# The X form of a blockwise triangular inverse kept in PSUM by an identity product, the other form added by VectorE

## What is computed

```
def step(S, inp):
    r_t, w_t, k_t, v_t, kk_t, a_t = inp
    sa = jnp.einsum('bhvk,bhk->bhv', S, -kk_t)
    S = S * w_t[:, :, None, :] + sa[..., None] * (kk_t * a_t)[:, :, None, :] + v_t[..., None] * k_t[:, :, None, :]
    return S, jnp.einsum('bhvk,bhk->bhv', S, r_t)
```

## Time and profile before

| | us |
|---|---|
| median of 3 runs (870.77 to 873.72) | 873.22 |
| the profiled execution itself | 872.92 |
| its span, first to last instruction | 871.1 |
| PE busy | 815.2 |
| DVE busy | 494.8 |
| ACT busy | 330.9 |
| RWKV stage, 222.9 to 357 us of the span | 134.1 |

### The profile page before, as it was taken

One profiled execution on the slowest core, in us unless ns is written; L12 is line 12 of the kernel. 1 busy time (PEld: TensorE's weight loads), 2 busy tenths in 40 slices (PEclk: granted clock), 3 DMA queues, 4 the chain that ended last, 5 costly groups with the idle time before them and its releaser, 6 DMA issues.

```text
span 871.1 us, 23141 instructions
## 1 busy us (share of the span) xinstructions
PE 815.2 (94%) x10012; PEld 763.6 (88%) x10012; DVE 494.8 (57%) x764; ACT 330.9 (38%) x569; POOL 274.0 (31%) x121
## 2 busy tenths in 40 slices
PE   6999999999887777899998999999999999999994
PEld 6899889898677676688888999999999999999994
DVE  5588766786577666265354777766667661000037
ACT  5644565454313122433265434333333331111124
POOL 0000000000297670325252444444344434344300
PEclk9999999999999999999998999999999999999997
DMA  7232133152243343703111333223322332333202
GB/s 267 84 97 74 49 98 98 49 198 61 88 116 107 107 126 118 237 15 104 58 54 44 98 113 106 80 91 98 97 86 85 98 88 89 92 88 89 85 2 99
DMA packets 32470, 83.47 MB, mean 96 GB/s; under 512 B 5144, under 2 KB 10456, under 8 KB 31728
## 3 DMA queue, kind: packets, MB, share of 16 engines
q1 hardware_dynamic: 32368, 81.98, 30.7%
HBM read 75.87 MB, written 5.91 MB: 94 GB/s over the span
## 4 chain that ended last, share of the span: by engine, by line
PE 86%; DVE 7%; ACT 3%; issue 2%; POOL 1%; DMA 0%; DVEq 0%; ACTq 0%; POOLq 0%
PE banks L1850 83%; PE banks L1904 1%; DVE z L1241 1%; DVE xx L1241 1%; PE banks L2253 1%; DVE ms L1241 1%; DVE rw L1241 1%; DVE z L1244 1%; POOL wr_lo L697 1%; DVE ssa L1505 1%; ACT x_hi L1149 0%; ACT z L1152 0%; ACT z L1212 0%; DMA w_raw<-in_w 0%; ACT nv L982 0%
## 5 line engine op out<-in xcount | busy, mean ns | idle before, releaser
L1850 PE MATMUL banks<-x_hi,w_hi 128*128 128x264 f32 (+1 forms) x784 | 207.7, 298 | 11.4 <-DVE x_lo L1241 8.9
L1850 PE MATMUL banks<-x_hi,w_lo 128*128 128x264 f32 (+1 forms) x784 | 198.3, 286 | 0.0
L1850 PE MATMUL banks<-x_lo,w_hi 128*128 128x264 f32 (+1 forms) x784 | 198.3, 286 | 0.0
L1850 PEld LDWEIGHTS banks<-x_hi,w_hi 128*128 128x128 f32 x784 | 138.9, 191 | 24.5 <-issue 11.3
L1850 PEld LDWEIGHTS banks<-x_lo,w_hi 128*128 128x128 f32 x784 | 139.1, 192 | 0.1
L1850 PEld LDWEIGHTS banks<-x_hi,w_lo 128*128 128x128 f32 x784 | 138.9, 191 | 0.0
L697 POOL TENSOR_TENSOR w_lo<-w_raw,w_hi 128x1024 fp32r<-128x1024 f32 (+1 forms) x38 | 90.6, 2385 | 152.2 <-ACT w_hi L825 152.0
L697 POOL TENSOR_TENSOR wx_lo<-w_raw,wx_hi 128x1024 fp32r<-128x1024 f32 (+1 forms) x34 | 81.8, 2406 | 100.5 <-ACT wx_hi L825 100.1
L1244 DVE SCALAR_TENSOR_TENSOR z<-z,banks 128x260 f32<-128x260 f32 (+1 forms) x24 | 12.4, 515 | 122.1 <-PE banks L1850 121.9
L1850 PE MATMUL banks<-x_hi,wx_lo 128*128 128x260 f32 x352 | 73.5, 283 | 0.0
L1850 PE MATMUL banks<-x_hi,wx_hi 128*128 128x260 f32 x352 | 73.5, 282 | 0.0
(11 more groups left out here) (254 smaller groups left out, 1713.0 us busy)
## 6 DMA issues: line engine op xcount, KB each, us to landing
w_raw<-in_w SPq DMA_DIRECT2D x87, 512.0 KB, 3.6
w_raw<-in_w SPq DMA_DIRECT2D x16, 448.0 KB, 3.3
kv<-in_ck SPq DMA_DIRECT2D x16, 192.0 KB, 4.1
kv<-in_cv SPq DMA_DIRECT2D x16, 192.0 KB, 3.4
att<-in_x SPq DMA_DIRECT2D x8, 264.0 KB, 6.0
att_out<-att SPq DMA_DIRECT2D x1, 2112.0 KB, 8.9
z<-in_xc SPq DMA_DIRECT2D x2, 1040.0 KB, 6.7
y_out<-z SPq DMA_DIRECT2D x8, 260.0 KB, 2.2
```

Of the source, the lines that this page charges most:

```text
L1850: return pe.matmul(out, l, r, start=start, stop=stop)
```

## The change

The masks of levels 1 to 5 change sign, so that the update adds where it subtracted. On PE a new `keep(n, l, g)` stands right after both groups of `half_products`, for l = 1..4: for each partition half j one matmul of the identity with form 1 of four heads (256 columns) starts an accumulation in bank 4g+1; the level's form-1 products are then added to it there. DVE's `update` treats only form 0 (128x256). ACT's new `x_copy(n, l)` copies form 1 back, 128x256 per group. At l = 5 nothing of this kind is kept, and DVE's `xf` waits for the copy. The copies are put into ACT's list; the `vb` activations (L1032), `ssoft`, `sprob` and `wu_copy` keep their order, with copies between. Four semaphores are merged into others: `zeroed` for two zeroing flags, `bsel_landed` counts `own_head` too, and `sel_landed` counts `gate_up`, so that `gate(0)` waits for three transfers and not one.

```
+    lev[:, 1:NLEV] *= -1
...
+        def x_copy(n, l):
+            for g in range(2):
+                ac.wait_ge(d_ps, (NLEV - 1) * 2 * n + 2 * (l - 1) + g + 1)
+                ac.activation(xx[:, 4 * g:4 * g + 4, 1, :], banks[:, 4 * g + 1, 256:512].rearrange("p (h s) -> p h s", h=4),
+                              ACT.Copy).then_inc(xg_done, 1)
+                own(xg_done)
...
-        for tb in range(1, TB):
-            vt_copy(tb)
+        vt_copy(1)
+        x_copy(0, 1)
+        vt_copy(2)
+        vt_copy(3)
+        for l in range(2, NLEV - 1):
+            x_copy(0, l)
...
                 b1_copy(n - 1)
+                x_copy(n, 1)
...
                 wu_copy(n - 1)
+                x_copy(n, 2)
+                if n == TB - 1:
+                    ac.wait_ge(s_pback, 1)
...
+                x_copy(n, 3)
                 if n == 1:
                     for c in range(CC):
...
                     token_copy(n, 0)
+                x_copy(n, 4)
                 ny_copy(n - 1)
...
-                x = xx[:, hs, :, :].rearrange("p h a s -> p a h s")
-                tt(x, x, banks[:, 4 * g:4 * g + 2, 256:512].rearrange("p a (h s) -> p a h s", h=4), ALU.subtract)\
+                tt(xx[:, hs, 0, :], xx[:, hs, 0, :], banks[:, 4 * g, 256:512].rearrange("p (h s) -> p h s", h=4), ALU.add)\
                     .then_inc(d_done, 1)
             else:
+                ve.wait_ge(xg_done, 2 * (NLEV - 2) * (n + 1))
...
-                   ALU.subtract).then_inc(d_done, 1)
+                   ALU.add).then_inc(d_done, 1)
...
+        def keep(n, l, g):
+
+            if l > 1:
+                pe.wait_ge(xg_done, 2 * ((NLEV - 2) * n + l - 2) + g + 1)
+            for j in range(2):
+                mm(banks[rows(j), 4 * g + 1, 256:512], level[rows(j), NLEV, :], xx[rows(j), 4 * g:4 * g + 4, 1, :], True, False)
...
-                    ins = mm(banks[rows(j), 4 * g + 1, o], lower[rows(j), h, 1, :], xx[rows(j), h, 1, :])
-                    if l < NLEV - 1:
+                    ins = mm(banks[rows(j), 4 * g + 1, o], lower[rows(j), h, 1, :], xx[rows(j), h, 1, :], last, last or i == 3)
+                    if not last:
...
                     half_products(n, l)
+                if l < NLEV - 1:
+                    keep(n, l, 0)
+                    keep(n, l, 1)
...
-                pe.wait_ge(gate_landed, 16)
+                pe.wait_ge(sel_landed, 48)
```

More of the change, by code:

```diff
@@ L127, in shape_constants @@
     lev[:, NLEV] = k[:, None] == t[None, :]
+    before, upto = k[:, None] < t[None, :], k[:, None] <= t[None, :]
+    lev[:, 1:NLEV] *= -1
     c["level"] = lev
-    before, upto = k[:, None] < t[None, :], k[:, None] <= t[None, :]
     c["causal"] = np.concatenate([before, upto, before, -lev[:, 0]], 1).astype(np.float32)
@@ L333, in layer @@
     late_landed = sem("late_landed")
-    gate_landed = sem("gate_landed")
     bsel_landed = sem("bsel_landed")
-    own_landed = sem("own_landed")
     x_hi_ready = sem("x_hi_ready")
@@ L340, in layer @@
     rw_ready = sem("rw_ready")
-    pre_zero = sem("pre_zero")
+    zeroed = sem("zeroed")
     v_tok_ps = sem("v_tok_ps")
@@ L354, in layer @@
     att_left = sem("att_left")
-    kv_zero = sem("kv_zero")
     s_rows_ps = sem("s_rows_ps")
@@ L413, in layer @@
     d_done = sem("d_done")
+    xg_done = sem("xg_done")
     b1_ps = sem("b1_ps")
@@ L542, in keys_of @@
             r = b % NKV
-            sp.wait_ge(kv_zero, min(b, NKV - 1) + 1)
+            sp.wait_ge(zeroed, min(b, NKV - 1) + 2)
             if b >= NKV:
@@ L608, in _ @@
         sp.wait_ge(n_spread, CC)
-        sp.dma_start(low_up[:], a["own_head"]).then_inc(own_landed, 16)
+        sp.dma_start(low_up[:], a["own_head"]).then_inc(bsel_landed, 16)
         sp.wait_ge(w_hi_ready, N_IN)
@@ L647, in _ @@
         sp.wait_ge(att_left, 16)
-        sp.dma_start(gate_up[:], a["gate_up"]).then_inc(gate_landed, 16)
+        sp.dma_start(gate_up[:], a["gate_up"]).then_inc(sel_landed, 16)
         sp.dma_start(gsel[:], a["gsel"]).then_inc(sel_landed, 16)
@@ L699, in w_low @@
             own(w_late_ready)
-        pool.memset(pre[:, :, 0:1], 0.0).then_inc(pre_zero, 1)
-        own(pre_zero)
+        pool.memset(pre[:, :, 0:1], 0.0).then_inc(zeroed, 1)
+        own(zeroed)
         pool.wait_ge(slot_used, N_IN)
         for r in range(NKV):
-            pool.memset(kv[96:P, r * NSB * AW:(r + 1) * NSB * AW], 0.0).then_inc(kv_zero, 1)
-            own(kv_zero)
+            pool.memset(kv[96:P, r * NSB * AW:(r + 1) * NSB * AW], 0.0).then_inc(zeroed, 1)
+            own(zeroed)
         def products(b):
@@ L826, in late_high @@
             own(w_hi_ready)
-        ac.wait_ge(pre_zero, 1)
+        ac.wait_ge(zeroed, 1)
         ac.activation(pre[:, 1, 0:1], pre[:, 1, 0:1], ACT.Copy)
@@ L1028, in _ @@
                 wu_copy(n - 1)
+                x_copy(n, 2)
+                if n == TB - 1:
+                    ac.wait_ge(s_pback, 1)
+                    ac.activation(sprob[:, :, :], banks[:, 7, 0:NSB * B * H].rearrange("p (t n) -> p t n", t=NSB),
+                                  ACT.Copy).then_inc(s_prob, 1)
+                    own(s_prob)
+                x_copy(n, 3)
                 if n == 1:
@@ L1493, in own_heads @@
         def own_heads(g):
-            ve.wait_ge(own_landed, 16)
+            ve.wait_ge(bsel_landed, 32)
             ve.wait_ge(s_pv, NSB * (g + 1))
@@ L2061, in inverse_scores @@
                 pe.wait_ge(p_done, 2 * (NLEV - 1) * n - 1 + g)
+                pe.wait_ge(xg_done, 2 * (NLEV - 2) * n - 1 + g)
             for i in range(2):
@@ L2137, in full_products @@
             pe.wait_ge(p_done, k + 1)
-            if l == NLEV - 1 and n + 1 < TB:
+            last = l == NLEV - 1
+            if last:
+                pe.wait_ge(xg_done, 2 * (NLEV - 2) * n + 2 * (NLEV - 2) - 1 + g)
+            if last and n + 1 < TB:
                 pe.wait_ge(sc_ps, 2 * n + g + 3)
@@ L2411, in gn_spread @@
             if u == 0:
-                pe.wait_ge(sel_landed, 32)
+                pe.wait_ge(sel_landed, 48)
             pe.wait_ge(n_inv, RT_G + u + 1)
```

## The result

The median after is 876.43 us (874.61 to 879.25, 17 runs) against 871.47 (867.81 to 874.91, 17 runs) for the kernel before: ratio 1.0057, 95% interval [1.0043, 1.0071], slower by 5.0 us. The forecast was 879.2, slower by 6.0 than the 873.2 of the runs shown then. The profiled execution took 878.41, 5.5 more than that of before (872.92); both are slower than their kernel's median, by 2.0 and 1.5 us.

A forecast was written before the change was run, and what follows sets the result against it. It took a dependency chain hopping between PE and DVE as the stage's bound. Added 11.4 us minus 5.1 gained gave +6.3, less 0.2 for a stall: 873.2 + 6.1, say 879.2 us; range 870.0 to 882.5.

The forecast's parts named there:

- What bounds the stage: A dependency chain hopping between PE and DVE; the end of PE's inserted key_scores and value_scores releases DVE's masks.
- Price of `keep`: Identity products on PE behind the half products, ahead of the inserted work: 0.85 us per level, 11.4 us in all.
- The gain: Shorter DVE updates after levels 1, 2, 3: 0.27 + 0.54 + 0.54 per step n = 1 to 3; 5.1 us in all.
- n = 0: First step: keep adds 2.43 us over levels 1 to 4; levels 1 and 2 gain 0.54 each.
- Level 4 of n = 1: PE restarts at a low clock after 2.71 us idle and is itself the bound; keep costs 1.3 us there.
- The stall: A 0.43 us issue stall between level 2's two groups; added pauses may shrink it, so 0.2 us taken off.
- Rival 1: Levels 1 to 3: keep is covered on free array quarters and only the gain remains, 868 us; chance 0.15.
- the forecast's second rule: PSUM evacuation: using both ScalarE and VectorE is advised; by it the sum would be the 5.1 us gain alone.
- Rival 2: Low-clock stretches: added PE work keeps the clock up, saving 4.7 us at most, no change at 873.8; chance 0.12.
- Rival 3: keep costs double, from quarters in turn or a new low-clock stretch per step: about 21 us, 889; chance 0.06.
- ACT's copies and the merged waits: 32 ACT copies, 12.3 us of ACT work, and gate(0) waiting for three transfers: cost 0 on the path.

The follow-up runs named there:

- The late version: The changed kernel with keep moved from behind the half products to just ahead of the full products; 0.9997 of the kernel before, 872.32 us.
- `keep` alone: The kernel before with keep's identity products added behind the half products, their result overwritten, DVE and ACT unchanged; ratio 1.0098, 881.40 us.
- the gain alone: The changed kernel without keep, so the inverse is not computed; ratio 0.9975 to the kernel before, 870.43 us.
- the shifted runs: Tiny products at kernel start: kernel before with 32, 876.11 us, with 64, 873.35; changed kernel with 32, 879.37; with keep also ahead of full products, 879.52.

## Why the prediction was right, and which terms were off

- **What bounds the stage.** Right: the release of the masks by PE's inserted work, ahead of the updates. The late version shows it by taking 0.83 us back at the mask with the same work on PE. (The 0.022 us a record that the forecast worked out from the earlier trace rows counts only the 95 records on the chain; the stretch holds 113, so 0.018. It supports the same conclusion, that the quarters run side by side.)
- **Price of `keep`.** 0.85 us a level was taken from the identity products of the start; measured 0.83 at level 1. Exposed at level 1 and 2, as forecast. From level 2 to 3 the sum of price and gain should have been 0.85 - 0.54 = +0.31 and was +0.16, so 0.7 of the 0.85 was exposed there, as the 0.68 of `keep` alone says too. Alone, the price was 8.5 us and not 11.4.
- **The gain.** 0.27 + 0.54 + 0.54 a step: shown at level 4 (-0.52, the forecast's -0.54) and in the gain alone (0.26, 0.52 and 0.52). So a step of n >= 1 should come to +1.20 by the forecast (1.35 gained, 2.55 added) and came to +1.07.
- **n = 0.** +1.35 forecast (2.43 less 1.08), +0.88 measured.
- **Level 4 of n = 1.** 1.3 us for work at half clock. This term failed as put: the low stretch it rests on was not there. The same view of after at 272.2 us, and at two other stretches:

```profile
272.20:279.00 6.80, 5.49 (x255) 4.91 (x256) 5.34 (x11) 4.48 (x8) 6.52 (x3) 1.00 0.14 44
...
284.00:287.00 3.00, 3.00 (x62) 2.67 (x62) 1.02 (x2) 0.64 (x2) 0.00 (x0) 0.50 0.69 217
...
356.00:360.00 4.00, 4.00 (x61) 3.55 (x59) 2.13 (x7) 1.92 (x3) 3.49 (x2) 0.50 1.08 316
```

  The granted clock at 272.2 is 1.00 (2.4 GHz) and is 0.50 (1.2 GHz) later, at 284, after a stretch in which PE stood still for issue and for DVE, and again at 356, behind the 3.95 us stall. In the stage as a whole it is 0.95, where the earlier trace rows have 0.96. What level 4 of n = 1 cost can't be read, since a stall (0.49) lies in it.
- **The stall.** The forecast knew of one, of 0.43 us, and took 0.2 off for "added pauses before it". This step failed: the chain of before had 5.8 us of such pieces in the stage, and the profiled execution of after 9.95. They are no pause that shrinks but late instruction blocks, and adding 128 PE and 128 PEld records to the stage moved their boundaries. Moved boundaries alone do not explain the rise: the last stall lies at nearly the same place in both (318 records before the output projection in before, 324 in after) and took 3.95 us instead of 2.71. That the time came out so near the forecast (+5.0 for +6.0) is in part luck: the measured levels gave +4.1 where the forecast had +5.0 for them (its +6.3 less the 1.3 of level 4 of n = 1), and stalls and clock, for which it had nothing like their size, can move a version by 3 us and more, as the shifted runs show.
- **Rivals.** Rival 1 (`keep` covered, 868) falls by the row of 2.88 against 2.05; the gain alone, which this rival and the forecast's second rule would leave, is not what came. The Trainium skill ("TensorEngine Tiling (Array Packing)", section PSUM Bottleneck) advises to use both ScalarE and VectorE for evacuation. Here that freed DVE of 8.4 us, and by itself, without `keep`, it took 2.2 us off; the identity products that it needs for a right result cost more. Rival 2 (the clock stays up) falls by the rows just shown: added PE work did not keep the clock up. The Trainium skill ("TensorE: Matmul & The Clock Gate", Part 1) says that activity releases the throttle; the trace agrees only in that both low stretches follow idle time of PE (1.73 and 3.95 us of issue). Rival 3 (889) falls: `keep` cost what one row said.
- ACT's copies and the merged waits cost nothing that shows, as forecast: the waits of PE in the stage of after name no ACT `xx`, and from the output projection on both kernels take 511 us.

## What to carry to other kernels

Ask what releases the next engine before adding work to an engine that has idle time: 0.83 us of work ahead of the release cost 0.83 us at level 1 and 0.7 at level 3, and the same work behind it cost nothing at level 1. Where PE is itself the bound, as in step n = 0, the place does not help. An instruction that starts a PSUM accumulation with an identity saves a vector operation but is paid on TensorE, and 4 records of 256 columns on one array quarter cost more (0.83) than the shorter update gave back (0.27 to 0.54) at each place. Where a stage issues small matmuls densely, measure a change at two block alignments (a half block of dummy instructions where the engine waits anyway) before believing a difference under 0.5%: half a block alone moved before by 0.34%.

## What the runs showed of the hardware that was not expected

PE's instruction list arrives in blocks of 256 instructions, 16 KB each, and PE stood still for up to 4.16 us at a block's end. Nothing in the trace of before said that 128 instructions at the kernel's start, in time that PE waited anyway, would cost 3.0 us 250 us later, and 256 instructions none. The late packets of the longest stalls began after PE had stopped; what starts a packet, and so which of the 28 blocks of the stage come late and by how much, stays open. Traffic on the transfer queues does not explain it alone: the 2.71 us stall of before has a DMA share of 1.03 in the view by stretch:

```profile
348.22:350.92 2.70, 0.00 (x0) 0.00 (x0) 0.00 (x0) 2.61 (x7) 0.00 (x0) 1.00 1.03 266
```

The longer one, 4.16 us, in before with half a block, has 0.22:

```profile
299.30:303.45 4.15, 0.00 (x0) 0.00 (x1) 1.21 (x2) 0.00 (x0) 3.99 (x3) 1.00 0.22 82
```

A version with fewer PE instructions in the stage, which would test whether the rate of issue is the cause, was not tried.
